# Attention and compression work moved between the tiles of the second input projection, and one compression block moved among the memory steps of layer 0

## The chip, the cores and the metric

The program runs on one core of one Trainium2 chip. Its time is the device time in microseconds; lower is better. TensorE (PE) multiplies, and its weight loads (PEld) run beside the products; VectorE (DVE), ScalarE (ACT) and GpSimd (POOL) do the rest; SyncE (SP), ACT and POOL start DMAs. All data are float32, and one matrix product of float32 leaves two records in the trace, a transpose one.

## The reference

One step of a decoder with two layers, for a prompt of 256 tokens and 8 samples of 4 new tokens (T = 288 columns together). In both layers a token mixer runs beside a four-head attention into 256 memory tokens; one projection feeds both, one projection closes them, and a SwiGLU channel mixer follows.

```python
mkv_p = mem_kv_proj(mem_prompt, w_mem_kv[i])
hp = rmsnorm(xp, norm_mix_pre[i])
if i % N_MIXERS == 0:
    mp, hl_p = s5_mixer(hp, h0_p, mkv_p, ...)      # z = hp @ w_in, then a complex scan over time
else:
    mp, (kc, ks, kw) = nsa_prompt(hp, mkv_p, ...)
    ms, (sc, ss, sw) = nsa_sample(hs, mkv_s, ...)
xp = xp + rmsnorm(mp @ w_out[i], norm_mix_post[i])
xp = xp + rmsnorm(swiglu_ffn(rmsnorm(xp, norm_ffn_pre[i]), ...), norm_ffn_post[i])
```

The second layer's attention has three branches, added with gates that the projection gives. For a sample they are:

```python
proj = cmp_subblock_proj(past_cmp, w1)             # 8 x 2048 cached rows, from pages
ckv = cmp_tokens(proj, pe, w1, b1, w2)             # 127 compressed tokens each
o_cmp, p = cmp_attend(q, q_pos, ckv, slopes)
tok = block_tokens(select_blocks(p, q_pos, total)) # 16 blocks of 64 cached rows
o_slc = slc_attend(q, q_pos, tok, kv_sel, slopes)  # over the selected cached rows
o_win = win_attend(q, q_pos, kv_w, k_pos, slopes)  # over the last 512 rows
```

## The kernel before

Each engine has its own instruction stream, written out by hand in program order, and semaphores join them. Nothing is reordered at run time: an instruction that waits holds up all that stands behind it on its engine. The eight PSUM banks (BK) are kept by a small class: `banks.fill(pe, key, b)` makes TensorE wait until bank b was read, `banks.take(eng, key)` makes a reader wait until it is full, and `wait_given` waits until a reader has let it go.

`gemm` computes one projection tile by tile: a tile is 128 output columns by 288 tokens, 8 products (16 records), and after tile number i it calls `hook(i)`. The weights come in slabs of two tiles through three slots of `W_`. `IN_ORDER` gives the order of the tiles: in layer 1 the tiles 15 and 16 are the memory queries, 0 to 5 the queries, 6 to 8 the rows to be compressed, 9 to 14 keys and values, 17 the gates. VectorE evacuates each tile (`in_evac`), scaled by the norm's inverse root, which it computes by a reciprocal after `pre_sum(4)`, and `pre_sum(4)` stands after the second tile. Layer 0 uses banks 4 and 5 for the tiles (`bank45`), layer 1 banks 4, 5 and 6 (`bank456`). `mem_step(l, zq, n)`, n = 0 to 9, is the attention into the memory in ten steps, put between the tiles.

Layer 0. After the projection come `s5_blocks` (L644), memory steps 7 (L583), 8 (L595) and 9 (L605) with `cmp_bias` (L652), then sixteen blocks `compress(b, c)` (L694, 16 products, 32 records each), which compress the cached pages of the samples for layer 1. Between the blocks stand `s5_in(n)` (L664) and `s5_y(n)` (L677) for the 15 units of the scan, whose other parts run on VectorE and GpSimd. SyncE loads the pages of sample b into half b % 2 of the buffer `AR` (16 DMAs, L2010); the first half also held `PEP`, the scratch of the position products that GpSimd sums for `cmp_bias`, and so SyncE waits for `pe_summed` first. The second half is free once memory step 8 is through (`("mo", 0, 2)`).

Layer 1. After the projection's 18 tiles come, on TensorE: the gates' transposes (L834), `compress_prompt` (L849, 64 products, 128 records), the row gates (L861), transposes of values (L868), the compressed tokens (L874, L879), scores of the prompt against them (L892), and transposes of their probabilities (L902). Then a loop over 12 units of the prompt's attention (scores L922, transposes L933, products with the values L946 to L953), with one of 12 groups of page scores (`page_scores(c, h)`, L967) of the samples in each unit. Behind the loop stand the samples' own rows (L986, L992), their compressed scores (L998), window scores (L1007), importance (L1012), transposes (L1017, L1025, L1060) and the products with values (L1039): first compressed and window values, which end in `win_used`, then four pairs of samples with the values of their pages, and last the output transposes (L1087).

Key pages come in four chunks c, each 16 DMAs on SyncE and 16 on GpSimd (L397), into two halves of `AR` (`KP`); chunk c waits until the page scores of chunk c - 2 are through. Value pages come in eight batches b of 16 DMAs (L403), even b on SyncE, odd b on GpSimd, each into its place `VAL[b]` when `wait_value_slot` says that it is free. Window keys `WK` (L2060) and values `WV` (L2062) take halves of `AR` too.

## Time and profile before

| | us |
|---|---|
| runs, median of 3 | 1201.52 |
| runs, all | 1195.62, 1201.52, 1202.44 |
| the profiled execution, its own time | 1197.44 |
| its span | 1195.8 |
| TensorE busy in the span | 1109.1 (93%) |

The span is what the profiler saw from the first to the last instruction; 1.6 us lie around it. The mean granted TensorE clock is 0.958 of its full rate. The projections, the compression and the two channel mixers are long stretches in which TensorE has no gap. Its gaps lie in the stretch from 70 to 85 us of layer 0, and between 704 and 884 us of layer 1.

### The profile page before, as it was taken

How to read it: one execution, taken by the hardware profiler on the slowest of the kernel's cores; microseconds unless marked ns; L12 is line 12 of the kernel's file. 1: busy time of each engine (PE TensorE's matmuls, PEld its weight loads, DVE VectorE, ACT ScalarE, POOL GpSimd, SP SyncE). 2: the span in 40 equal slices, each digit the busy share in tenths (PEclk: the TensorE clock that was granted, in tenths of full speed). 3: DMA queues.
4: the chain of work that ended last, by engine and by line, in shares of the span. 5: the costliest groups of instructions: out<-in, count | busy, mean ns of one | idle time of the engine just before them, and what ended most of it. 6: DMA issues, size and time to landing. Idle time of an engine off the chain costs nothing.

```text
span 1195.8 us, 16402 instructions
## 1 busy us (share of the span) xinstructions
PE 1109.1 (93%) x6032; PEld 810.3 (68%) x6032; DVE 366.4 (31%) x789; ACT 202.5 (17%) x497; POOL 242.1 (20%) x314
## 2 busy tenths in 40 slices
PE   6979999999989999999999996884888999999996
PEld 5746666666767777777767774443766777777774
DVE  5728677430142111100032104777213211110002
ACT  3310000012231000000031103554103100000000
POOL 0608567620001111130000031414400110110000
PEclk9979999999999999999999996897879999999998
DMA  8565434330425656674433344575723244333341
GB/s 321 211 211 172 144 120 121 106 107 8 175 71 186 238 217 245 263 252 153 156 141 106 109 147 125 156 267 146 211 86 122 106 141 140 130 127 113 130 145 64
DMA packets 59112, 185.13 MB, mean 155 GB/s; under 512 B 8609, under 2 KB 39586, under 8 KB 48418
## 3 DMA queue, kind: packets, MB, share of 16 engines
q1 hardware_dynamic: 52322, 165.28, 40.2%
q0 software_dynamic: 6144, 12.59, 3.6%
q10 hardware_dynamic: 576, 6.29, 1.4%
q8 instruction: 48, 0.79, 0.3%
q14 instruction: 22, 0.18, 0.0%
HBM read 180.35 MB, written 10.02 MB: 159 GB/s over the span
## 4 chain that ended last, share of the span: by engine, by line
PE 87%; DVE 4%; issue 2%; SPq 2%; DMA 2%; ACT 1%; POOLq 0%; POOL 0%; DVEq 0%
PE banks L718 29%; PE banks L496 16%; PE banks L758 14%; PE banks L694 14%; PE banks L516 3%; SPq L397 1%; PE banks L664 1%; PE banks L1039 1%; PE banks L849 1%; PE banks L677 1%; PE banks L562 1%; PE banks L1060 1%; SPq L393 1%; DMA phase<-in_slcv 1%; PE banks L471 1%
## 5 line engine op out<-in xcount | busy, mean ns | idle before, releaser
L718 PE MATMUL banks<-normed,slabs 128*128 128x288 f32 x1408 | 346.6, 410 | 9.1 <-ACT normed L1140 9.1
L718 PEld LDWEIGHTS banks<-normed,slabs 128*128 128x128 f32 x1408 | 270.1, 192 | 85.2 <-issue 10.0
L758 PE MATMUL banks<-hidden,slabs 128*128 128x288 f32 x704 | 171.2, 406 | 1.4 <-issue 1.4
L694 PE MATMUL banks<-arena,phase 128*128 128x384 f32 x512 | 171.7, 494 | 0.0
L758 PEld LDWEIGHTS banks<-hidden,slabs 128*128 128x128 f32 x704 | 133.6, 190 | 39.0 <-issue 2.3
L694 PEld LDWEIGHTS banks<-arena,phase 128*128 128x128 f32 x512 | 96.9, 192 | 65.4 <-issue 1.8
L1425 POOL TENSOR_TENSOR projected<-projected,rstd 128x288 f32<-128x288 f32 x44 | 34.9, 792 | 449.3 <-ACT projected L1207 449.3
L496 PE MATMUL banks<-normed,slabs 128*128 128x288 f32 (+1 forms) x416 | 106.6, 410 | 1.2 <-ACT normed L1140 1.2
L496 PEld LDWEIGHTS banks<-normed,slabs 128*128 128x128 f32 (+1 forms) x416 | 75.7, 187 | 27.1 <-issue 3.7
L1509 DVE TENSOR_TENSOR normed<-normed 128x288 f32<-128x288 f32 x24 | 11.0, 459 | 199.0 <-ACT normed L1200 199.0
L1207 ACT ACTIVATE projected<-projected 128x288 f32<-128x288 f32 x44 | 19.5, 443 | 281.4 <-DVE projected L1556 281.4
L496 PE MATMUL banks<-mixed,slabs 128*128 128x288 f32 x256 | 64.3, 414 | 1.3 <-DVE mixed L1942 1.3
L1561 DVE TENSOR_TENSOR hidden<-projected,banks 128x288 f32<-128x288 f32 x44 | 20.0, 454 | 138.8 <-PE banks L718 130.1
L496 PEld LDWEIGHTS banks<-mixed,slabs 128*128 128x128 f32 x256 | 49.7, 195 | 15.3 <-issue 1.4
L1556 DVE TENSOR_TENSOR projected<-banks,rstd 128x288 f32<-128x288 f32 x44 | 20.1, 457 | 127.8 <-PE banks L718 127.7
L1200 ACT ACTIVATE normed<-banks 128x288 f32<-128x288 f32 x32 | 13.1, 410 | 251.0 <-PE banks L758 164.2
L397 POOL DMA_DIRECT2D arena<-in_slck x64 | 33.3, 521 | 101.5 <-issue 97.2
L516 PE MATMUL banks<-slabs,mixed 128*128 128x256 f32 x128 | 30.6, 402 | 8.9 <-DMA slabs<-in_w 8.9
L1462 POOL TENSOR_TENSOR phase_small<-normed,phase 128x512 f32<-128x512 f32 (+1 forms) x15 | 17.1, 1141 | 91.9 <-DVE normed L1702 62.0
L1517 DVE RECIPROCAL rstd<-rstd 128x288 f32<-128x288 f32 x8 | 15.6, 1953 | 62.9 <-ACT rstd L1131 62.9
L516 PEld LDWEIGHTS banks<-slabs,mixed 128*128 128x128 f32 x128 | 26.0, 204 | 12.9 <-issue 8.8
L403 POOL DMA_DIRECT2D arena<-in_slcv x32 | 20.1, 630 | 43.2 <-issue 41.7
(293 smaller groups left out, 1071.7 us busy)
## 6 DMA issues: line engine op xcount, KB each, us to landing
slabs<-in_wfi SPq DMA_DIRECT2D x44, 1024.0 KB, 4.9
slabs<-in_w SPq DMA_DIRECT2D x25, 1024.0 KB, 4.8
arena<-in_cmp SPq DMA_DIRECT2D x128, 192.0 KB, 2.7
slabs<-in_wfo SPq DMA_DIRECT2D x32, 704.0 KB, 4.1
arena<-in_slck SPq DMA_DIRECT2D x64, 96.0 KB, 2.7
arena<-in_slck POOLq DMA_DIRECT2D x64, 96.0 KB, 2.5
out_win_old<-in_winold SPq DMA_DIRECT2D x8, 762.0 KB, 6.3
arena<-in_wink SPq DMA_DIRECT2D x4, 768.0 KB, 6.5
```

Of the source, the lines that this page charges most:

```text
L397: eng.dma_start(AR[lo:lo + 64, a:a + 384], page(slck_in, r)).then_inc(kpage_loaded[c % 2][parity], 16)
L403: eng.dma_start(dst, page(slcv_in, r)).then_inc(vpage_loaded[b], 16)
L496: ins = nc.tensor.matmul(BK[b][0:n_out, 0:T], wt[:, k, c * P:c * P + n_out], rhs[:, k, :], start=(k == 0), stop=(k == kc - 1))
L516: ins = nc.tensor.matmul(BK[b][:, 0:256], MEMT[:, k, t * P:t * P + P], wt[:, k, :], start=(k == 0), stop=(k == KC - 1))
L694: ins = nc.tensor.matmul(out.rearrange("p h (g s) -> p h g s", s=8), W1S[:, c, a, j, :], PG[b % 2][:, :, c * 8 + j, :, :].rearrange("p g h ...
L718: return nc.tensor.matmul(BK[2 * (u % SLOTS) + c][:, 0:T], wt[:, k, c * P:c * P + P], Hn[:, k, :], start=(k == 0), stop=(k == KC - 1), ski ...
L758: ins = nc.tensor.matmul(BK[b][:, 0:T], wt[:, k, :], HD[:, 11 * kh + k, :], start=(kh + k == 0), stop=(kh * 11 + k == 21))
L1207: A(z, z, ACT.Silu).then_inc(silu_done, 1)
L1425: tt(z, z, RST[:, :], ALU.mult).then_inc(up_done, 1)
L1462: ch.tick(tt(hr, re, cos, ALU.mult))
L1556: banks.give(tt(z, BK[2 * (u % SLOTS)][:, 0:T], RST[:, :], ALU.mult), key)
L1561: banks.give(tt(HD[:, u, :], z, BK[2 * (u % SLOTS) + 1][:, 0:T], ALU.mult), up)
```

## The change

**Layer 0.** `compress` calls `between(i)` ahead of each product but the first. Block (0, 0) now begins right after `s5_blocks`, and memory steps 7, 8, 9 and `cmp_bias` stand between its products. `s5_in(0)` follows it. `s5_in(n)` for n over 1 stands one block later than before in the count of blocks, `s5_in(1)` in the middle of block 1, and the last `s5_y` in the middle of the last block. `PEP` lies in `M_`, in twelve tiles that are summed step by step, and SyncE no longer waits for `pe_summed` before the first pages.

**Layer 1.** The tiles come in the order 15, 16, 6, 7, 8, 0 to 5, 17, 9 to 14. Between them stand the memory steps and now also `compress_prompt`, the compressed tokens and their scores and transposes, the gates, and the samples' compressed scores, window scores, importance and transposes. Banks 6 and 7 serve them, and the tiles have banks 4 and 5 (`bank45`). VectorE and ScalarE have the matching work in between. In the unit loop stand, new, the window's maximum and exponentials (units 0 and 1), its scaling (unit 2) and its five transposes (`window_turn`, units 3 to 7, in bank 7 with the page scores). The selected rows' probabilities are transposed head by head, with more of it overlapped with the exponentials.

**DMAs of layer 1.** Window keys come during the first channel mixer. Key chunk 0 waits for memory step 8 of layer 1, chunk 1 for the window scores, chunks 2 and 3 as before. Value batch 0 waits for the last `window_turn`, batches 1 and 2 for the last page scores (before, batches 0 and 1 waited for the last slabs of the projection alone), 3 to 5 for `win_used`, 6 and 7 for the transposes of the selected rows. On SyncE the window values stand behind value batch 0.

```diff
-IN_ORDER = [[6, 7, 0, 1, 2, 3, 4, 5], [15, 16] + list(range(15)) + [17]]
+IN_ORDER = [[6, 7, 0, 1, 2, 3, 4, 5], [15, 16, 6, 7, 8, 0, 1, 2, 3, 4, 5, 17] + list(range(9, 15))]
...
-        PEP = AR[:, 2048:6144].rearrange("p (c q f) -> p c q f", c=2, q=16)
+        PEP = M_[:, 0:1536].rearrange("p (n f) -> p n f", f=P)
...
-        KP = [AR[:, a:a + 6144].rearrange("p (b g h n) -> p b g h n", b=4, g=4, h=H) for a in (6144, 0)]
-
-        VAL = [W_[:, 0:3072], W_[:, 3072:6144]] + [AR[:, a:a + 3072] for a in (6144, 9216, 0, 3072)] + [KV[:, :], U[:, 0:3072]]
+        KP = [AR[:, a:a + 6144].rearrange("p (b g h n) -> p b g h n", b=4, g=4, h=H) for a in (0, 6144)]
+
+        VAL = [W_[:, 3072:6144]] + [AR[:, a:a + 3072] for a in (6144, 9216)] + [KV[:, :]] + [AR[:, a:a + 3072] for a in (0, 3072)]
+        VAL += [U[:, a:a + 3072] for a in (0, 3072)]
...
             if c >= 2:
                 banks.take(eng, ("sk", c - 2, H - 1))
             elif c == 1:
+                for h in range(H):
+                    banks.take(eng, ("sws", h))
+            else:
                 banks.take(eng, ("mo", 1, 2))
-            else:
-                banks.take(eng, ("hc", B - 1, 1))
-            lo, base = 64 * parity, 6144 * (1 - c % 2)
-            for b in pairs:
+            lo, base = 64 * parity, 6144 * (c % 2)
+            for b in range(4):
...
-            if b < 2:
-                for n in range(FIRST["out", 1] - SLOTS, FIRST["out", 1]):
-                    eng.wait_ge(*released[n])
-            elif b < 4:
-                for h in range(H):
-                    banks.take(eng, ("sws", h))
-            elif b < 7:
+            if b == 0:
+                banks.take(eng, ("swt", 4))
+            elif b < 3:
+                banks.take(eng, ("sk", 3, H - 1))
+            elif b < 6:
                 eng.wait_ge(win_used, 1)
             else:
                 banks.take(eng, ("st", NPG))
...
             s5_blocks()
-            mem_step(0, 6, 7)
-            cmp_bias()
-            mem_step(0, 6, 8)
+
+            def beside_first(i):
+                if i == 6:
+                    mem_step(0, 6, 7)
+                elif i == 7:
+                    cmp_bias()
+                elif i == 9:
+                    mem_step(0, 6, 8)
+                elif i == 13:
+                    mem_step(0, 6, 9)
+
+            compress(0, 0, between=beside_first)
             for r in range(2):
                 for part in range(2):
                     banks.wait_given(pe, ("bt", r, part))
             for m in range(8):
                 banks.wait_given(pe, ("in", 0, m))
-            mem_step(0, 6, 9)
             for key in (("ms", 0, 4), ("ms", 0, 3), ("mto", 0), ("mo", 0, 2)):
                 banks.wait_given(pe, key)
             pe.wait_ge(smat_loaded, 32)
             s5_in(0)
-            for blk in range(2 * B):
+
+            def beside_block(blk, i):
+                if i == 8 and blk == 1:
+                    s5_in(1)
+                elif i == 8 and blk == 2 * B - 1:
+                    s5_y(N_UNIT - 1)
+
+            for blk in range(1, 2 * B):
                 b, c = blk // 2, blk % 2
-                compress(b, c, halfway=lambda: s5_in(1) if blk == 0 else None)
+                compress(b, c, between=lambda i: beside_block(blk, i))
-                for n in outputs_beside(blk):
-                    s5_y(n)
-                if blk + 2 < N_UNIT:
-                    s5_in(blk + 2)
+                for n in outputs_beside(blk - 1):
+                    if n < N_UNIT - 1:
+                        s5_y(n)
+                if blk + 1 < N_UNIT:
+                    s5_in(blk + 1)
...
-                if i == 1:
-                    pre_sum(4)
-                if 3 <= i <= 12:
-                    mem_step(1, 15, i - 3)
-
-            gemm("in", 1, Hn, KC, N_NSA_SLAB, IN_ORDER[1], ready=lambda k: pe.wait_ge(h_done, 16 + k + 1), cols=36,
-                 bank=bank456, hook=beside_in)
-            banks.wait_given(pe, ("in", 1, 17))
...
+                if i == 1:
+                    pre_sum(4)
+                if 3 <= i <= 12:
+                    mem_step(1, 15, i - 3)
+                if 5 <= i <= 8:
+                    compress_prompt(i - 5)
+                if i == 9:
+                    prompt_tokens()
+                if i == 11:
+                    prompt_cmp_scores()
+                if i == 12:
+                    gates_turn()
+                    sample_cmp_scores()
+                if i == 13:
+                    row_gates()
+                if i == 14:
+                    window_scores()
+                    prompt_cmp_turn(0)
+                    prompt_cmp_turn(1)
+                if i == 15:
+                    importance()
+                    prompt_cmp_turn(2)
+                    prompt_cmp_turn(3)
+                if i == 16:
+                    sample_cmp_turn()
+                    prompt_cmp_turn(4)
+                    prompt_cmp_turn(5)
+
+            gemm("in", 1, Hn, KC, N_NSA_SLAB, IN_ORDER[1], ready=lambda k: pe.wait_ge(h_done, 16 + k + 1), cols=36,
+                 bank=bank45, hook=beside_in)
...
+                if 3 <= n < 8:
+                    window_turn(n - 3)
...
+                if n == 1:
+                    row_exp(lambda h: SW[:, h, :], 3, sw_max, 1, sw_exp)
...
+                if i == 10:
+                    query_rows()
+                if i == 11:
+                    prompt_cmp_scored()
+                if m >= 9 and m < 15:
+                    upper_keys(m)
+                if i == 12:
+                    prompt_cmp_prob()
+                    sample_cmp_scored()
+                if i == 13:
+                    row_gates_out()
+                    sample_cmp_prob()
+                if i == 15:
+                    selection()
             for g in range(G):
...
+                    ch.step(V.tensor_reduce(NEWMAX, SNEW, AX_X, ALU.max))
+                    V.tensor_reduce(NS[:, 3:6], SW, AX_X, ALU.max, negate=True).then_inc(sw_max, 1)
...
-            sp.wait_ge(pe_summed, 1)
             load_pages(0)
...
-                    load_key_pages(sp, SP, 0, 0, [u // 2])
+                    a = 6144 + 1536 * (u // 2)
+                    sp.dma_start(AR[:, a:a + 1536], wink_in[u // 2]).then_inc(wink_loaded, 16)
             load_stage("mem", 1, N_MEM_SLAB)
-            load_stage("in", 1, N_NSA_SLAB)
+            for u in range(N_NSA_SLAB):
+                load(FIRST["in", 1] + u)
+                if u == 3:
+                    store_mem_kv(1)
+            load_key_pages(sp, SP, 0, 0)
+            load_key_pages(sp, SP, 1, 0)
             for m in range(6, 15):
                 banks.wait_given(sp, ("in", 1, m))
             sp.dma_start(kv_out, Z_[:, 6 * T:15 * T]).then_inc(kv_stored, 16)
-            store_mem_kv(1)
-            sp.wait_ge(memkv_stored, 32)
-            load_key_pages(sp, SP, 1, 0)
+            load_key_pages(sp, SP, 2, 0)
+            load_key_pages(sp, SP, 3, 0)
             wait_value_slot(sp, 0)
             load_value_pages(sp, SP, 0)
-            for c in range(2, 4):
-                load_key_pages(sp, SP, c, 0)
             banks.take(sp, ("sk", 2, H - 1))
-            for b in range(4):
-                a = 6144 + 1536 * b
-                sp.dma_start(AR[:, a:a + 1536], wink_in[b]).then_inc(wink_loaded, 16)
-            banks.take(sp, ("sk", 3, H - 1))
             sp.dma_start(AR[:, 0:6144], winv_in).then_inc(winv_loaded, 16)
...
-            load_key_pages(pool, POOL, 0, 1)
             banks.take(pool, ("fo", 0, KC - 1))
             query_blocks(1, 15)
-            load_key_pages(pool, POOL, 1, 1)
-            wait_value_slot(pool, 1)
-            load_value_pages(pool, POOL, 1)
-            for c in range(2, 4):
+            for c in range(4):
                 load_key_pages(pool, POOL, c, 1)
-            for b in range(3, B, 2):
+            for b in range(1, B, 2):
                 wait_value_slot(pool, b)
                 load_value_pages(pool, POOL, b)
             channel_mixer(1)
```

TensorE in layer 0, from `s5_blocks` (L644) on; the products of `compress` are the rows with `128x3x128`. Before:

```order
L644 MATMUL banks<-cst,cmp_kv 128x128 x12
L583 MATMUL banks<-cst,hidden 128x128 x2
L652 MATMUL banks<-cst,phase_small 128x1 x2
L595 MATMUL banks<-arena,hidden 32x128 x32
L605 MATMUL banks<-cst,hidden 128x128 x4
L664 MATMUL banks<-projected,hidden 128x64 x16
L694 MATMUL banks<-arena,phase 128x3x128 x8
L664 MATMUL banks<-projected,hidden 128x64 x16
L694 MATMUL banks<-arena,phase 128x3x128 x8
```

and now:

```order
L645 MATMUL banks<-cst,cmp_kv 128x128 x12
L695 MATMUL banks<-arena,phase 128x3x128 x6
L584 MATMUL banks<-cst,hidden 128x128 x2
L695 MATMUL banks<-arena,phase 128x3x128
L653 MATMUL banks<-cst,phase_small 128x1 x2
L695 MATMUL banks<-arena,phase 128x3x128 x2
L596 MATMUL banks<-arena,hidden 32x128 x32
L695 MATMUL banks<-arena,phase 128x3x128 x4
L606 MATMUL banks<-cst,hidden 128x128 x4
L695 MATMUL banks<-arena,phase 128x3x128 x3
L665 MATMUL banks<-projected,hidden 128x64 x16
L695 MATMUL banks<-arena,phase 128x3x128 x8
```

Block (0, 0) has moved from behind `s5_in(0)` (L664, now L665) to the place right behind `s5_blocks`, and the memory steps (L584, L596, L606) lie inside it.

TensorE in layer 1, the first four tiles of the projection (L496, now L497) with what they wait for; L471 (now L472) is `pre_sum(4)`. Before:

```order
L496 MATMUL banks<-normed,slabs 128x288 [waits normed_done,bank4_free,slab2_loaded]
L496 MATMUL banks<-normed,slabs 128x288 [waits normed_done] x7
L496 MATMUL banks<-normed,slabs 128x288 [waits bank5_free]
L496 MATMUL banks<-normed,slabs 128x288 x7
L471 MATMUL banks<-projected,cst 128x288 [waits squares_summed,bank7_free]
L496 MATMUL banks<-normed,slabs 128x288 [waits bank6_free,slab0_loaded]
L496 MATMUL banks<-normed,slabs 128x288 x7
L496 MATMUL banks<-normed,slabs 128x288 [waits bank4_free]
L496 MATMUL banks<-normed,slabs 128x288 x7
```

and now:

```order
L497 MATMUL banks<-normed,slabs 128x288 [waits normed_done,bank5_free,slab2_loaded]
L497 MATMUL banks<-normed,slabs 128x288 [waits normed_done] x7
L497 MATMUL banks<-normed,slabs 128x288 [waits bank4_free]
L497 MATMUL banks<-normed,slabs 128x288 x7
L472 MATMUL banks<-projected,cst 128x288 [waits squares_summed,bank7_free]
L497 MATMUL banks<-normed,slabs 128x288 [waits bank5_free,slab0_loaded]
L497 MATMUL banks<-normed,slabs 128x288 x7
L497 MATMUL banks<-normed,slabs 128x288 [waits bank4_free]
L497 MATMUL banks<-normed,slabs 128x288 x7
```

The third tile waited for bank 6, which no earlier tile had filled; now it waits for bank 5, that of the first tile.

SyncE in layer 1, around the window values. Before, they stand behind the window keys and ahead of value batch 2:

```order
L2060 DMA arena<-in_wink 128x1536 [waits bank7_full]
L2060 DMA arena<-in_wink 128x1536 x3
L2062 DMA arena<-in_winv 128x6144 [waits bank7_full]
L400 UNCONDITIONAL_BRANCH [waits bank4_full,bank3_full,bank2_full]
L400 ISA
L361 TENSOR_LOAD pages
L361 ISA x8
L403 ISA
L403 DMA arena<-in_slcv 128x192
```

and now, from the last DMA of a group of value batch 0 on:

```order
L406 DMA slabs<-in_slcv 128x192
L403 REGISTER_ALU
L403 COMPARE_AND_BRANCH
L2172 DMA arena<-in_winv 128x6144 [waits bank7_full]
L403 UNCONDITIONAL_BRANCH [waits bank7_full]
L403 ISA
L363 TENSOR_LOAD pages
L363 ISA x8
L406 ISA
L406 DMA arena<-in_slcv 128x192
```

Value batch 0 has moved in ahead of the window values, behind the last key pages.

## Rows read from the trace of the kernel before

**Rows 1.** The page's chain that ended last: shares of the span by engine.

```profile
PE 87%; DVE 4%; issue 2%; SPq 2%; DMA 2%; ACT 1%; POOLq 0%; POOL 0%; DVEq 0%
```

**Rows 2.** Waits of TensorE, whole span: total us, times, longest us.

```profile
PE banks L1060 <- DVE phase L1924: 9.6, 3, 4.0
...
PE banks L902 <- DVE params L1786: 5.6, 1, 5.6
```

**Rows 3.** Timeline of TensorE, layer 0: start us, duration us, line, idle before.

```profile
72.68 0.44 PE L583 MATMUL banks<-cst,hidden 128*128 128x128 f32 x2 [1.78 <-DVE hidden L1547]
...
77.80 1.94 PE L595 MATMUL banks<-arena,hidden 128*32 128x128 f32 x32 [3.12 <-DMA arena<-in_memv]
...
84.69 7.49 PE L694 MATMUL banks<-arena,phase 128*128 128x384 f32 x16
...
98.51 1.12 PE L664 MATMUL banks<-projected,hidden 32*128 32x64 f32 x32
...
99.56 10.59 PE L694 MATMUL banks<-arena,phase 128*128 128x384 f32 x32
```

**Rows 4.** Timeline of SyncE's DMA issues, layer 0.

```profile
25.86 9.30 SPq L1978 DMA_DIRECT2D slabs<-in_w  x2
...
59.26 15.47 SPq L2010 DMA_DIRECT2D arena<-in_cmp  x16
...
81.56 14.90 SPq L2010 DMA_DIRECT2D arena<-in_cmp  x16
```

**Rows 5.** Stretches of 1 us, L849 alone: PE busy, PEld busy, PEclk, DMA.

```profile
711.00:712.00 1.00, 1.00 (x22) 1.00 (x22) 1.00 0.05 16
...
716.00:717.00 1.00, 1.00 (x13) 1.00 (x12) 0.50 0.43 121
```

**Rows 6.** Timeline of VectorE at the second projection's first tiles.

```profile
632.85 1.96 DVE L1517 RECIPROCAL rstd<-rstd 128x288 f32<-128x288 f32 x1 [4.84 <-ACT rstd L1131]
...
634.83 0.82 DVE L1568 SCALAR_TENSOR_TENSOR projected<-banks,rstd 128x288 f32<-128x288 f32 x2
```

**Rows 7.** Timeline of TensorE, layer 1, projection to window scores.

```profile
632.11 7.92 PE L496 MATMUL banks<-normed,slabs 128*128 128x288 f32 x32
...
708.76 9.59 PE L849 MATMUL banks<-projected,phase 64*128 64x45 f32 x128
...
739.78 0.34 PE L922 MATMUL banks<-projected 64*128 64x128 f32 x1 [1.18 <-ACT hidden L1305]
...
749.95 1.59 PE L967 MATMUL banks<-arena,phase 128*32 128x512 f32 x8
...
786.47 1.06 PE L967 MATMUL banks<-arena,phase 128*32 128x512 f32 x8 [0.37 <-DMA arena<-in_slck]
...
801.27 0.83 PE L986 MATMUL banks<-cst,projected 128*32 128x128 f32 x6
...
804.66 2.76 PE L1007 MATMUL banks<-arena,phase 128*32 128x512 f32 x24
```

**Rows 8.** Timeline of SyncE's DMA issues, layer 1.

```profile
729.08 13.98 SPq L403 DMA_DIRECT2D slabs<-in_slcv  x16
...
753.13 31.42 SPq L397 DMA_DIRECT2D arena<-in_slck  x32
```

**Rows 9.** DMA issues by line: KB each, median us to landing.

```profile
arena<-in_winv SPq DMA_DIRECT2D x1, 3072.0 KB, 10.1
```

**Rows 10.** Timeline of GpSimd, issues of the last value pages.

```profile
848.24 2.47 POOL L403 DMA_DIRECT2D phase<-in_slcv  x4 [2.62 <-issue]
...
860.87 2.47 POOL L403 DMA_DIRECT2D phase<-in_slcv  x4 [1.74 <-issue]
```

**Rows 11.** Timeline of TensorE, value products of layer 1.

```profile
822.04 5.41 PE L1039 MATMUL banks<-arena,hidden 128*48 128x192 f32 x64
...
870.15 0.53 PE L1039 MATMUL banks<-cmp_kv,hidden 128*48 128x192 f32 x1 [5.74 <-DMA phase<-in_slcv]
```

More of the change, by code:

```diff
@@ new lines, in importance, with sample_cmp_turn @@
+            def importance():
+                pe.wait_ge(imp_done, 1)
+                banks.fill(pe, "imp", 3)
+                banks.filled(nc.tensor.matmul(BK[3][:, 0:96], c2("same"), IMP[:, :, 0:32], start=True, stop=True), "imp")
+            def sample_cmp_turn():
+                pe.wait_ge(sc_prob, 1)
+                banks.wait_given(pe, "imp")
+                banks.fill(pe, "sct", 3)
+                for h in range(H):
+                    ins = nc.tensor.transpose(BK[3][0:NCMP, P * h:P * h + P], PC[:, h, 0:NCMP], ident)
+                banks.filled(ins, "sct")
@@ L905, in _ @@
+            for j in range(6):
+                ins = nc.tensor.matmul(BK[4][:, 32 * j:32 * j + 32], Q0[0:64, j % 3, :], Z[0:64, 9 + j, TP:T], start=True, stop=True)
+            banks.filled(ins, "snew")
             for n in range(6):
@@ new lines, in _ @@
+                ins = V.tensor_copy(dst, src.rearrange("p h (b t) -> p h b t", b=B))
+                if g < 3:
+                    ch.step(ins)
+            ins.then_inc(q_done, 1)
+            for h in range(H):
+                banks.take(dve, ("sws", h))
+                banks.give(stt(SW[:, h, 0:WIN], c2("win_d"), slope[:, h:h + 1], BK[h][:, :], ALU.mult, ALU.add), ("sws", h))
+            banks.take(dve, "snew")
+            for j in range(6):
+                dst = SNEW[:, j, :] if j < 3 else SW[:, j - 3, WIN:WIN + 32]
+                ins = stt(dst, c2("new_d"), slope[:, j % 3:j % 3 + 1], BK[4][:, 32 * j:32 * j + 32], ALU.mult, ALU.add)
+                if j < 5:
+                    ch.tick(ins)
+                else:
+                    banks.give(ins, "snew")
@@ L1925, in _ @@
[L1925 to L1927 removed]
+                if n == 2:
+                    dve.wait_ge(sw_exp, 1)
+                    ch.step(V.reciprocal(SS[:, 3:6], SS[:, 3:6]))
+                    ch.step(tt(SS[:, 3:6], SS[:, 3:6], GR[:, 6:9], ALU.mult))
+                    for h in range(H):
+                        ins = ts(SW[:, h, :], SW[:, h, :], SS[:, 3 + h:4 + h], None, ALU.mult)
+                        if h < 2:
+                            ch.tick(ins)
+                    ins.then_inc(sw_prob, 1)
@@ new lines, in slc_prob, with slc_turned @@
+            def slc_prob(h):
+                dve.wait_ge(ss_exp, h + 1)
+                ch.step(V.reciprocal(SS[:, h:h + 1], SS[:, h:h + 1]))
+                ch.step(tt(SS[:, h:h + 1], SS[:, h:h + 1], GR[:, 3 + h:4 + h], ALU.mult))
+                ts(S_SLC[:, h, :], S_SLC[:, h, :], SS[:, h:h + 1], None, ALU.mult).then_inc(ss_prob, 1)
+            def slc_turned(h):
+                for q in range(1, 4, 2):
+                    banks.take(dve, ("st", h, q))
+                    dst, src = turned_tiles(h, q)
+                    banks.give(V.tensor_copy(dst, src), ("st", h, q))
```

598 lines of the change are left out of this document (298 added, 300 removed).

## The prediction, made blind

> **What bounds the kernel now.** The page's chain that ended last comes first: 87% of it is TensorE, DVE, issue and DMA have 2 to 4% each [rows 1]. So an edit pays only where it removes a wait of TensorE, shortens TensorE's own work, or shortens a transfer for which TensorE waits. TensorE is busy for 1109.1 us of 1195.8. The waits of TensorE by partner show where to look: 9.6 us for the probabilities of the selected rows and 5.6 us for those of the prompt's compressed tokens [rows 2]. Then the timelines: layer 0 from 70 to 100 us [rows 3, 4], the second projection with what follows it [rows 5 to 7], and the chain of page DMAs up to the last value products [rows 7 to 11].
>
> **Layer 0.** Both kernels reach the end of `s5_blocks` alike, at 72.68 - 1.78 = 70.9. Before, block 1 begins at 99.56 [rows 3]: 28.7 us, in which stand block (0, 0), memory steps 7 to 9, `cmp_bias` and three calls of `s5_in`. TensorE idles in it for 1.8 us ahead of step 7 and for 3.1 ahead of step 8 (memory values landing), and some 2 us more around them. The first half of the block, 16 records, takes 7.49 us, where a whole block of 32 takes 10.59 later, so it runs at less than full rate too. The same work without gaps, at the later rate: 10.59 for the block, 3 x 1.12 for `s5_in` (two of these now stand later, but they still count), 0.44 for step 7, 1.94 for step 8 (its row, perhaps too high, as it follows a gap), and 1.0 for step 9 and `cmp_bias` (small products, by the same rows). That is 17.3, so 28.7 - 17.3 = **11.3 us gained**.
>
> What must hold for it. The pages of sample 0 must be there at 71: SyncE is through with the slabs at 25.86 + 9.30 = 35, and 16 pages take 15.5 to issue [rows 4]; as `pe_summed` no longer holds them, they end at about 54. Step 7 wants what VectorE gives at 72.6; with six products of 0.66 ahead of it, it comes at 74.9. Step 8 wants the memory values, which land at 77.8; it comes at about 78.6, behind nine products. This margin is 1 us. The second half of the pages waits for step 8, now done at about 81.4; with 14.9 of issue [rows 4] and some 2.6 to land it is whole at 99. Blocks 0 and 1 end at 88.2 + 11.7 = 99.9, a margin of 1 again, and a miss costs the difference, up to 3. The scan keeps its distance, three blocks from `s5_in(n)` to `s5_y(n)`, and the last output has half a block, 5.3, to hide it. The summing of `PEP` on GpSimd goes to another buffer in the same steps: nothing. The term is 8 to 12.
>
> **Layer 1, the projection.** Five parts.
> First, a new wait. With two banks the third tile waits until VectorE has evacuated the first, and that needs the reciprocal, done at 632.85 + 1.96 = 634.8, and half of 0.82 [rows 6]: 635.3, where it began at 632.11 [rows 7]. 3.2 us. TensorE has stood for some microseconds then, and it may start at the lower of its two levels; the bound is 0 to 3, and I take 2.5, since rows after other gaps do so. Together +5.7.
> Second, `compress_prompt` takes 9.59 us for 128 records [rows 7]. In its first microseconds the granted clock is 1.00 and 22 records fit in one, later it is 0.50 and 13 fit in one, with PE and PEld both fully busy [rows 5]. Between full tiles I expect the first: 128/22 = 5.8, so -3.8.
> Third, from its end at 718.35 to the loop's first scores at 739.78 there are 21.4 us. The waits of 5.6 [rows 2] and 1.2 [rows 7] go: -6.8.
> Fourth, the rest, 14.6, runs at the lower level. At the full one it takes between 7.3 (all of it clocked) and 14.6; I take 9: -5.7.
> Fifth, what comes in from behind the loop: the window scores, 2.76 [rows 7], compressed scores, samples' rows, importance and transposes, some 3.4, and half a microsecond of waits for banks 6 and 7: +6.7.
> Sum: 5.7 - 3.8 - 6.8 - 5.7 + 6.7 = -3.9. The loop begins at 735.9.
>
> A rule of the Trainium skill speaks against the second and fourth parts. The page "TensorE: Matmul & The Clock Gate", section "HAM oscillation — how this bites in real kernels", puts the loss of clock down to gaps in which TensorE idles. By that rule alone small products back to back would keep the full clock wherever they stand, and moving them would not bring those 9.5 us; the clock in the row for 716 us, where no gap is, does not bear it out [rows 5]. By the rule the projection part would come out at +5.6 and not at -3.9.
>
> **Layer 1, from the loop on.** Now the page DMAs count. In the loop VectorE gets the window's maximum (1632 wide, about 2.1 in unit 0) and the scaling in unit 2; I add 0.6 up to the end of the page scores of unit 2. That end is 749.95 + 1.59 = 751.5 now, 11.8 behind the loop's start [rows 7], and 748.3 after. Call it P2; from it the distances are fixed by issuing:
> - chunks 2 and 3 are issued from P2 + 1.6 for 31.4 [rows 8], up to P2 + 33; the scores of unit 9 wait for them at P2 + 35, as before [rows 7]; the loop ends at P2 + 49.8 (801.27 now), and I keep that;
> - behind them SyncE now issues value batch 0, 14.0 [rows 8], and only then the window values, at P2 + 47; they take 10.1 [rows 9]: P2 + 57.4;
> - TensorE, done with the loop at P2 + 50 and with little left that was not moved, waits there for 4 to 6 us, new. The window products take 5.4 to 8 (64 records take 5.41 [rows 11]): `win_used` at P2 + 65, about 813;
> - GpSimd has batch 1 from the last page scores, P2 + 43.7, on. A batch there is four groups of 4.2 (from 848.24 to 860.87 are three [rows 10]): 16.8. Batches 3, 5 and 7 wait for `win_used`: 65 + 2 x 16.8 = 98.6, then 12.6 to the last group, 2.5 for it, 2.6 to land: P2 + 117, that is **865.3**.
> Before, the last pair begins at 870.15, after 5.74 of idle [rows 11], though its last group was out at 863.3 [rows 10], 6.8 earlier. The slabs for the output projection were loading beside it. With the earlier place of window and value batches I take 2.6, the usual distance of the other groups; with 6.8 the pair begins at 869.5. So this part gives **4.5**, between 0 and 9. The 9.6 us for the selected probabilities [rows 2] may go, but only in front of this wait, so I book nothing for them; were the pages not last, they would be the gain.
>
> For that landing the page "DMA: Bandwidth & Descriptors" of the Trainium skill, section "Anatomy of one DMA — SWDGE (gpsimd) path", has a formula of a fixed 2.0 us and the bytes over 436 GB/s: an estimate of 2.2 for the 96 KB of such a page. The 6.8 of the trace is three times that, so the last transfer was not alone. With 2.2 for 2.6 the sum would move by 0.4.
>
> Nothing else in the diff touches the end; the channel mixers are unchanged. The window keys come during the first one, where DMA queues have room: nothing, and 2 us if that is wrong.
>
> **The sum.** -11.3 - 4.5 = -15.8: the profiled execution goes from 1197.44 to 1181.6. It lies 4.1 under the median; the mean of the three runs is 1199.9, and I predict against that: **1184**. Its own bounds, 8 and 12 for the first term, 0 and 9 for the second, with the spread of the runs, give 1177 to 1191.
>
> **The rivals.**
> - Better: the pages are not last. If the clock stays up through the projection (-10 and not -4) and the value pages take fewer than 16.8 a batch on GpSimd, the 9.6 us count as well: -22, 1178. For it: SyncE needs only 14.0 for a batch [rows 8]. Against it: GpSimd's own pitch is even over four groups [rows 10].
> - Layer 1 gives nothing: the last landing takes 6.8 again, or the projection gains nothing: the small products hold their clock down also between tiles, or the bank wait comes back with every tile. Layer 0 alone is -11: 1189.
> - Small products run at one rate wherever they stand, and only idle gaps lower the clock: then the second and fourth part of the projection give nothing, -15.8 + 9.5 = -6.3: 1194. For it: the clock was 1.00 at 711 us. Against it: 0.50 at 716, with no gap [rows 5]. This is what the clock page's rule, above, would make of it.
> - Layer 0 does not deliver: memory values or pages come 3 us late at each of both margins, and the clock stays low behind the gap: 4 to 5 gained, 1193 with a little less in layer 1.
> - Slower: the window values. Now they are issued while GpSimd's pages of batch 1 land, and three later batches hang on `win_used`. Should they take 31 us, like the 3 MB of the key chunks [rows 8], and not 10.1 [rows 9], `win_used` comes 21 later, the last pair at 886, and the sum is +16 - 11 = +5: 1205; with TensorE at its lower level in such a wait, 5 to 9 more, up to 1214. It decides from `win_used` at 829 on. Against it: one large transfer in few descriptors, and 16 us of slack.
>
> **How the numbers follow.** The forecast has 0.50, better 0.15, no gain in layer 1 0.15, one rate for small products 0.05, layer 0 late 0.07, slower 0.08. One per cent, 12 us, is about what a measurement of this kernel can tell from no change; that is 1188. Faster: 0.43 of the forecast's 0.50, all of the better case, 0.04 of the third: 0.62. Slower by 1% needs over 1212, 0.05 with what no case names. The rest is 0.33. The range goes from 1173, the better case with its spread, to 1197; it leaves out the slower case and tails.
>
> **What would show it.** Right: block (0, 0) directly behind `s5_blocks`, and no wait for `in_memv`; one idle time of 3 to 6 us ahead of the third tile, ended by VectorE; a granted clock near 1.00 through the projection; the scores of unit 9 waiting for `in_slck`; a wait for `in_winv` behind the loop; and the last pair waiting for `in_slcv` near 854 in the new time (865.3 - 11.3). Wrong: waits for `in_cmp` ahead of block 2, clocks of 0.5 between the tiles, `win_used` over 10 us later than P2 + 65, or last value products that wait for the probabilities and not for pages. Times of layer 1 in this text are on the old clock, without the 11.3 of layer 0.

## The result and the profile after

The changed kernel takes 1191.83 us in the median of 17 runs (1189.99 to 1196.2), the kernel before 1197.62 (17 runs, 1195.62 to 1203.32). The ratio is 0.9947, with a 95% interval of 0.9935 to 0.996: 6.3 us faster (4.8 to 7.8). The forecast gain was 16. The profiled execution took 1191.83 us with a span of 1190.2, against 1197.44 and 1195.8; the mean granted clock is 0.965 (0.958 before).

The timeline of TensorE, changed kernel, layer 0 (start us, duration, line, operation, idle before). Against them stand [rows 3].

```profile
71.33 4.04 PE L695 MATMUL banks<-arena,phase 128*128 128x384 f32 x12
...
77.90 1.95 PE L596 MATMUL banks<-arena,hidden 128*32 128x128 f32 x64
...
84.94 1.12 PE L665 MATMUL banks<-projected,hidden 32*128 32x64 f32 x32
...
279.60 17.68 PE L497 MATMUL banks<-projected,slabs 128*128 128x288 f32 x72
```

Block (0, 0) stands directly behind `s5_blocks`, step 8 waits for nothing, and the block is through at 84.94. The gated projection behind the blocks begins at 279.60. In the kernel before, this row of the same view is

```profile
290.68 17.68 PE L496 MATMUL banks<-projected,slabs 128*128 128x288 f32 x72
```

so layer 0 gave 11.1 us up to there. Before, the second projection begins at

```profile
621.94 9.85 PE L496 MATMUL banks<-normed,slabs 128*128 128x288 f32 x32 [1.20 <-ACT normed L1140]
```

The same view of the changed kernel in layer 1, from the second projection to the output projection; [rows 7, 11] answer to them.

```profile
611.92 9.85 PE L497 MATMUL banks<-normed,slabs 128*128 128x288 f32 x32 [1.20 <-ACT normed L1202]
...
625.41 9.69 PE L497 MATMUL banks<-normed,slabs 128*128 128x288 f32 x32 [3.16 <-DVE projected L1641]
...
646.09 2.00 PE L851 MATMUL banks<-projected,phase 64*128 64x45 f32 x32
...
690.56 5.83 PE L497 MATMUL banks<-normed,slabs 128*128 128x288 f32 x16
...
727.52 0.37 PE L1006 MATMUL banks<-hidden,projected 64*128 64x128 f32 x1
...
733.91 1.07 PE L1049 MATMUL banks<-arena,phase 128*32 128x512 f32 x8 [2.93 <-DVE phase L1969]
...
740.46 1.87 PE L1049 MATMUL banks<-arena,phase 128*32 128x512 f32 x8
...
804.27 6.72 PE L1094 MATMUL banks<-arena,slabs 128*48 128x192 f32 x64 [7.62 <-DMA arena<-in_winv]
...
852.65 8.11 PE L1094 MATMUL banks<-arena,hidden 128*48 128x192 f32 x64 [14.08 <-DMA arena<-in_slcv]
...
864.59 7.09 PE L1094 MATMUL banks<-phase,hidden 128*48 128x192 f32 x64 [3.37 <-DMA phase<-in_slcv]
...
878.10 27.18 PE L497 MATMUL banks<-mixed,slabs 128*128 128x288 f32 x103 [1.30 <-DVE mixed L2054]
```

The reader is to see: the idle time ahead of the third tile (625.41); four calls of `compress_prompt` of 2 us between tiles (the first is shown); one tile that takes 5.83 us where its neighbours take 4.15 (the granted clock is 0.76 from 690 to 697); the page scores of unit 2, P2, ending at 740.46 + 1.87 = 742.3; 7.6 us for the window values; and the last pair at 864.59. Before, it began at 870.15 [rows 11]. So of the 11.1 us of layer 0 only 5.6 reach the last pair: layer 1 took the rest back. Where, the queues show. SyncE's issues, changed kernel (start, time from the first to the last issue, count), beside [rows 8]:

```profile
743.94 32.14 SPq L400 DMA_DIRECT2D arena<-in_slck  x32
777.85 14.84 SPq L406 DMA_DIRECT2D slabs<-in_slcv  x16
792.91 0.36 SPq L2172 DMA_DIRECT2D arena<-in_winv  x1
795.04 32.80 SPq L406 DMA_DIRECT2D arena<-in_slcv  x32
829.77 13.91 SPq L406 DMA_DIRECT2D phase<-in_slcv  x16
```

and GpSimd's, the first group of batch 3 and the last of batch 7, beside [rows 10]:

```profile
813.17 2.47 POOL L406 DMA_DIRECT2D cmp_kv<-in_slcv  x4 [9.18 <-issue]
...
860.29 2.47 POOL L406 DMA_DIRECT2D phase<-in_slcv  x4 [1.75 <-issue]
```

GpSimd stands for 9.2 us ahead of batch 3, until the window products (804.27 + 6.72 = 811.0) are through, and then issues three batches one right behind the other. The chain of layer 1 is: page scores of unit 2, key pages, value batch 0, window values, window products, three batches on GpSimd, last pair. From the key pages on, the window products are all that TensorE has in it.

### The profile page after: what moved, and what is told of

Same layout as the page of the kernel before. It is cut to its first block, busy times and chain, and to the rows that moved or that the text cites. A ratio compares the mean times of both kernels' runs of the same rounds, so it can differ in the third digit from the quotient of the medians.

```text
span 1190.2 us, 16408 instructions
## 1 busy us (share of the span) xinstructions
PE 1102.9 (93%) x6032; PEld 806.8 (68%) x6032; DVE 366.9 (31%) x789; ACT 201.6 (17%) x496; POOL 241.7 (20%) x315
## 4 chain that ended last, share of the span: by engine, by line
PE 86%; issue 4%; SPq 3%; DVE 3%; DMA 2%; POOLq 1%; ACT 1%; POOL 0%; DVEq 0%
PE banks L719 29%; PE banks L497 16%; PE banks L759 14%; PE banks L695 14%; PE banks L517 3%; SPq L400 2%; PE banks L665 1%; PE banks L1094 1%; POOLq L363 1%; DMA arena<-in_winv 1%; PE banks L678 1%; PE banks L563 1%; SPq L406 1%; DVE rstd L1590 1%; SPq L396 1%
## 5 line engine op out<-in xcount | busy, mean ns | idle before, releaser
L497 PE MATMUL banks<-normed,slabs 128*128 128x288 f32 (+1 forms) x416 | 111.2, 424 | 4.4 <-DVE projected L1641 3.2
L497 PEld LDWEIGHTS banks<-normed,slabs 128*128 128x128 f32 (+1 forms) x416 | 78.9, 194 | 29.6 <-issue 6.4
L497 PE MATMUL banks<-mixed,slabs 128*128 128x288 f32 x256 | 64.4, 415 | 1.3 <-DVE mixed L2054 1.3
L497 PEld LDWEIGHTS banks<-mixed,slabs 128*128 128x128 f32 x256 | 49.8, 195 | 15.4 <-issue 1.4
L1262 ACT ACTIVATE normed<-banks 128x288 f32<-128x288 f32 x32 | 13.1, 410 | 270.5 <-PE banks L759 164.2
L1094 PE MATMUL banks<-arena,hidden 128*48 128x192 f32 x128 | 20.4, 396 | 17.7 <-DMA arena<-in_slcv 14.1
```

The lines of the kernel that those rows point to most:

```text
L497: ins = nc.tensor.matmul(BK[b][0:n_out, 0:T], wt[:, k, c * P:c * P + n_out], rhs[:, k, :], start=(k == 0), stop=(k == kc - 1))
L1094: return nc.tensor.matmul(out, probs[:, 48 * b:48 * b + 48], values, start=first, stop=last, skip_group_check=True)
```

## The experiments

Changes in us are the ratio times 1197.6. Intervals of the ratios are 0.0012 to 0.0019 to either side, 1.4 to 2.3 us, so a difference between two changed kernels is known to about 2.5 us. Where a difference to the changed kernel is given, it is one of two ratios to the kernel before.

**The two layers apart.** `l0_only` is the kernel before with the layer-0 hunks of the diff (`compress` with `between`, `beside_first`, `beside_block`, `PEP` in `M_`, no wait for `pe_summed`); `l1_only` is the changed kernel without them.

> The kernel before with the part of the change in layer 0 alone. Theory A (the two parts add up, and the profile reads layer 0 as 11.1 us and layer 1 as a loss of some 5 with the rest of the span): 10 to 11 us faster than before, ratio 0.991, with the layer-1 stretch moved as a whole. Rival B (the page DMAs of layer 1 do not care when layer 0 ends, or the clock gives part of it back): 6 us or less, as much as the whole change brings, so that layer 1 is neutral.

Measured: 0.9907 (0.9893 to 0.992), -11.1 us.

> The changed kernel with layer 0 as it was. Theory A: 4 to 5 us slower than before, ratio about 1.004, because the distance from the page scores of unit 2 to the last value pair grew from 118.7 to 122.3 us and the distance ahead of it did not shrink enough. Rival B: within 1 us of the kernel before.

Measured: 1.0031 (1.0019 to 1.0044), +3.7 us. Its span is 1.6 us longer than before, the smaller end of what the runs show. So layer 0 brings all of the gain and more, layer 1 is a loss; -11.1 + 3.7 = -7.4 agrees with -6.3 within the intervals. Rival B of both expectations is out.

**What the last pair hangs on.** Two kernels that differ from the changed one in one place each.

```diff
 # winv_first
+            banks.take(sp, ("sk", 2, H - 1))
+            sp.dma_start(AR[:, 0:6144], winv_in).then_inc(winv_loaded, 16)
             wait_value_slot(sp, 0)
             load_value_pages(sp, SP, 0)
-            banks.take(sp, ("sk", 2, H - 1))
-            sp.dma_start(AR[:, 0:6144], winv_in).then_inc(winv_loaded, 16)
```

> The changed kernel with the window values issued ahead of value batch 0 on SyncE. Theory A (window values set the time of win_used, and three batches of GpSimd hang on it): window values land at about 788 in place of 804, GpSimd goes from its batch 1 into batch 3 without a gap at about 805, and the last pair begins 7 us earlier, near 857.5: about 7 us faster than the changed kernel, ratio to before about 0.989. Rival B (TensorE's own work and the landing of pages under load set the end, not the issue): the window products come earlier and the last pair moves by 2 us or less.

Measured: 0.9881 (0.9865 to 0.9897), -14.3 us, 7.9 faster than the changed kernel. Its GpSimd and its TensorE:

```profile
801.32 2.47 POOL L406 DMA_DIRECT2D arena<-in_slcv  x4 [1.73 <-issue]
805.50 3.05 POOL L406 DMA_DIRECT2D cmp_kv<-in_slcv  x4 [1.71 <-issue]
```

```profile
796.65 5.41 PE L1094 MATMUL banks<-arena,slabs 128*48 128x192 f32 x64
...
857.35 6.97 PE L1094 MATMUL banks<-phase,hidden 128*48 128x192 f32 x64 [9.40 <-DMA phase<-in_slcv]
```

The window products wait for nothing, batch 3 follows batch 1 at once (805.50 where it was 813.17), and the last pair begins at 857.35, where 857.5 was expected. The chain starts 0.9 us earlier in this trace (P2 ends at 741.47), so 6.4 of the 7.2 us lie behind P2.

```diff
 # batch3_early
+            elif b == 3:
+                eng.wait_ge(kv_used, 1)
             elif b < 6:
                 eng.wait_ge(win_used, 1)
...
-                seq_pv(b, PCT[0:NCMP, :], VC[0:NCMP, b, :], first=b // 2 % 2 == 0)
+                ins = seq_pv(b, PCT[0:NCMP, :], VC[0:NCMP, b, :], first=b // 2 % 2 == 0)
+            ins.then_inc(kv_used, 1)
```

> The changed kernel with value batch 3 released by the compressed products alone (a semaphore of its own) and not by the window products. Theory A: GpSimd starts batch 3 at about 805 in place of 813, nothing else moves up to the window products, and the last pair begins 7 us earlier, ratio to before about 0.989, like the run that moves the window values. If instead the late landing of the window values matters in itself (theory C: TensorE stands 7.6 us for them and everything of TensorE behind comes later), this run gains little and that one gains.

Measured: 0.9902 (0.9887 to 0.9917), -11.7 us, 5.4 faster than the changed kernel; the last pair begins at 856.60. TensorE still idles 6.5 us for the window values there, and the last pair is as early as in `winv_first`: theory C is out. The gains of the two, 5.4 and 7.9 us, do not differ clearly. What counts is when GpSimd may go on, not when TensorE gets the window values.

**More of the same lever.** `swap_queues` has `for b in (0, 3, 5, 7)` on GpSimd, `for b in (1, 2, 4, 6)` behind the window values on SyncE, and `kv_used`.

> The changed kernel; GpSimd issues value batches 0, 3, 5 and 7 (batch 0 is free after the last window turn), SyncE the window values and then 1, 2, 4 and 6, and batch 3 waits for the compressed products alone. Theory A (issue slots decide): GpSimd begins batch 0 at 776 behind its key pages and ends batch 7 near 846, SyncE ends near 847, the last pair begins near 849 in place of 864.6: 15 us faster than the changed kernel, ratio to before about 0.982. Rival B (below some 857 the landing of 96 KB pages or TensorE's pairs take over): 857, as in the two runs with one edit, ratio 0.988.

Measured: 0.9854 (0.9837 to 0.9871), -17.5 us; the last pair begins at 854.40, between the two forecasts. GpSimd was through at 846.8, as theory A has it, but SyncE only at 838.70 + 13.90 = 852.6: three batches from 787.94 took 48.8 us, 16.3 each with the pauses between them, and not 14. The bound was again an issue queue, the other one. The next kernel, `balanced`, takes this up: `(0, 1, 3, 5)` and four pages of 7 on GpSimd, `(2, 4, 6)` and twelve pages of 7 on SyncE.

> The changed kernel with value batches 0, 1, 3, 5 and the first four pages of 7 on GpSimd, and the window values, 2, 4, 6 and the other twelve pages of 7 on SyncE; batch 3 waits for the compressed products alone. Theory A: with SyncE at 16.3 us a batch from 788 on (as the run with the swapped queues shows it) and GpSimd at 16.8 from 775 on, the last page is issued at about 849 on either queue and the last pair begins near 851: 13 to 14 us faster than the changed kernel, 3 us faster than the swapped queues, ratio to before 0.983. Rival B (what is left after the swap is not the issue but TensorE and the landing): no faster than the swapped queues, 0.985.

Measured: 0.9791 (0.9772 to 0.981), -25.0 us. Its TensorE:

```profile
843.21 7.06 PE L1097 MATMUL banks<-arena,hidden 128*48 128x192 f32 x64 [9.46 <-DMA arena<-in_slcv]
...
850.65 5.41 PE L1097 MATMUL banks<-phase,hidden 128*48 128x192 f32 x64
```

The last pair follows the third without idle time and runs at the full clock, 5.41 us where it took 7.09. The pair begins 13.9 us earlier than in the changed kernel, the output projection 16.1 earlier (862.00), and the ratios are 18.7 us apart, with intervals of 2 on each. The forecast time of the pair (851) was right, the ratio of 0.983 too high. The pair came at 851 for another reason than forecast: SyncE was through at 820.20 + 26.95 = 847.2, not 849, and the pair stood behind the third, which waits for batch 5 (9.46 us) and runs at a low clock. So the queues no longer alone decide; TensorE does in part.

**The wait ahead of the third tile.**

```diff
 # third_bank
+            first_tiles = [0]
+
+            def bank645():
+                first_tiles[0] += 1
+                return 6 if first_tiles[0] == 3 else bank45()
...
-                 bank=bank45, hook=beside_in)
+                 bank=bank645, hook=beside_in)
```

> The changed kernel with bank 6 for the third tile of the second projection, all others as they are. Theory A: the idle time of 3.2 us ahead of the third tile goes, and with it the 1.8 us by which that tile and the next run long; since the chain of page DMAs starts from the unit loop, all of the 5 us arrive at the end: 5 us faster than the changed kernel, ratio to before 0.990. Rival B (that stretch is covered, a later wait in the loop takes it): 1 us or less.

Measured: 0.9891 (0.9874 to 0.9909), -13.1 us, 6.7 faster than the changed kernel. The third tile in its trace:

```profile
620.49 7.92 PE L497 MATMUL banks<-normed,slabs 128*128 128x288 f32 x32
...
683.87 4.15 PE L497 MATMUL banks<-normed,slabs 128*128 128x288 f32 x16
```

From the first tile (610.32) it begins 10.2 us later, in the changed kernel 13.5. That is 3.3 for the wait; the lower clock behind it cost another 1.8 (7.92 against 9.69 for the same 32 records). A third part comes later: the tile at 690.56 that took 5.83 us takes 4.15 here (683.87). Up to the unit loop that makes 6.8 us (108.8 for 115.6). Whether the wait caused the slow tile too stays open: `l1_only` has the wait, 13.5 us from the first tile to the third, and not the slow tile (113.7 us up to the loop). From the first tile to the last pair it is 247.3 us (610.32 to 857.66) and not 252.7, so about the 5 us forecast arrive at the end of the chain; the measured 6.7 agrees with both within its interval.

> The balanced queues together with bank 6 for the third tile. Theory A: the two gains add up, as one lies ahead of the chain of page issues and the other in it: 6 to 7 us more than the balanced queues alone, ratio to before near 0.977 (1170.5 us). Rival B: they overlap by more than 3 us, 0.980 or above.

Measured: 0.9751 (0.9734 to 0.9769), 1169.6 us in the median, -29.8 us: 4.8 more than the balanced queues alone, with intervals of 2 on each. That is less than the forecast 6 to 7 but not clearly so, and rival B (0.980 or above) is out; in the traces the last pair comes 5.6 us earlier (845.10 for 850.65). It is the fastest kernel of the study, 23.5 us ahead of the changed one.

**The window's work in the unit loop.** `window_later` takes the maximum (L1997) behind the page scores of unit 1, and the exponentials, the scaling and the five `window_turn` one unit later each.

> The changed kernel with the maximum, exponentials, scaling and transposes of the window one unit later in the loop of units (the maximum after the page scores of unit 1). Theory A: TensorE's wait for bank 7 at unit 1 (2.9 us, ended by VectorE) goes by 2, the page scores of unit 2 end 2 us earlier, and the chain of issues and the last pair come 2 us earlier: ratio to before about 0.993. Rival B (VectorE is full in every unit of the loop, so the same work one unit later costs the same there): within 0.5 us of the changed kernel.

Measured: 0.9973 (0.9961 to 0.9985), 3.1 us slower than the changed kernel. Neither theory had this. Its SyncE and its GpSimd:

```profile
740.93 37.09 SPq L400 DMA_DIRECT2D arena<-in_slck  x32
```

```profile
763.63 2.35 POOL L400 DMA_DIRECT2D arena<-in_slck  x4 [8.77 <-PE banks L1060]
```

P2 did come earlier, 739.3 for 742.3, of which 1.3 are there from the first tile on (610.65), and chunk 2 came with it. But chunk 3 waits for the page scores of unit 5, and those now lay behind VectorE's scaling, a wait of 2.6 us in unit 4 and the lower clock behind it: they began at 759.71, in the changed kernel at 757.32. The two chunks took 37.09 us and not 32.14, and the chain behind them came later. So not P2 alone, but units 2 and 5 both hold the queue.

**The clock in small products.** `prompt_block` calls the four parts of `compress_prompt` together at i = 8; `prompt_two` calls two at i = 6 and two at i = 8.

> The changed kernel with the four parts of the prompt's compression, 128 records, together behind the ninth tile of the second projection, not in four places. Theory A (at the full clock these products need 22 records a microsecond, as before, and each of the four places costs a change-over of 0.4 us): 5.8 us from first to last start, about 1.5 us less than in four parts. Rival B (among full tiles they run at 17 a microsecond whatever the grouping): 7.3 us, nothing gained. Rival C: so long a run of small products pulls the granted clock down, and the block takes 9.6 us as before: 2 us slower than the changed kernel.

Measured: 0.9964 (0.995 to 0.9978), 2.0 us slower than the changed kernel, which is no more than its uncertainty; the traces have 118.2 us from the first tile to the unit loop where it was 115.6. The stretches of this line alone (TensorE busy, weight loads busy, granted clock, DMA share, GB/s):

```profile
665.00:666.00 1.00, 1.00 (x22) 1.00 (x22) 1.00 0.00 0
666.00:667.00 1.00, 1.00 (x20) 1.00 (x20) 0.86 0.00 0
667.00:668.00 1.00, 1.00 (x14) 1.00 (x12) 0.50 0.00 0
```

The block takes 9.68 us. Rival C is borne out: the clock falls from 2.4 to 1.2 GHz in the middle of it, at 666.7, with TensorE busy all the time; full tiles and 1.6 us of memory products stand right ahead. It is still low in the tile behind, which takes 6.74 us.

The numbers behind the x are not a rate. They count every record that runs in the stretch, also those that began before it, and at 1.00 one record takes 0.29 us: over the ten stretches of the whole block the counts add up to 169, for 128 records.

> The changed kernel with the prompt's compression in two stretches of 64 records, behind the seventh and the ninth tile. As one stretch of 128 between tiles the clock fell to 0.50 after some 4.5 us; as four of 32 it stayed at 1.00. If the small products themselves pull the clock down when they last long, two stretches of 64 (3 us each) still stay at 1.00 and take 6.2 us together; if the clock falls in them, over 7.5.

One run with a profile, 1190.27 us: 3.6 and 3.7 us from the start of each stretch to the next tile, at a granted clock of 1.00 throughout. The clock held, as in the first branch, but the sum is 7.3 and not 6.2. That is the true rate at 1.00: 64 records in 3.6 us, 56 ns each, or 17.7 in a microsecond. The 6.2, like the 22 of the first expectation, rests on the counts. The four parts of the changed kernel take 7.6 (646.09 to 648.02 is the first). So a change-over costs less than 0.2 us.

## Why the prediction was wrong, step by step

The direction was right and the time lies in the range of 1173 to 1197, but the gain is 6.3 us and not 16, and under the 1% to which I gave 0.62. Against 1184 the time is 7.8 us off and the gain 9.5, mainly because I predicted from the mean of three runs, 1199.9, and the kernel before has 1197.6 in 17. The bound was read rightly: TensorE, and in layer 1 the chain of page DMAs. Each step in its own order:

| step | forecast | measured |
|---|---|---|
| layer 0 | -11.3 | -11.1 (279.60 for 290.68); run alone -11.1 |
| start of the second projection | 610.6 | 611.92 |
| projection up to the unit loop | -3.9 | -2.2 (115.6 us for 117.8) |
| loop's start to P2 | 12.4 | 14.8 |
| P2 to the window values' issue | 47 | 50.6 |
| P2 to their landing | 57.4 | 61.9 |
| P2 to `win_used` | 65 | 68.7 |
| P2 to batch 3 on GpSimd | 65 | 70.8 |
| P2 to the last pair | 117 | 122.3 |

On the new clock the last pair was forecast for 854.0 and begins at 864.6. The 10.6 us are 1.3 + 1.7 + 2.4 + 5.3 (each rounded): the start of the projection, the projection, the loop to P2, and P2 to the last pair.

Three sums of the forecast do not come out. 98.6 + 12.6 + 2.5 + 2.6 is 116.3, not 117. From 865.3 to 870.15 are 4.9 us, not 4.5; with 116.3 it would have been 5.5, further from the result. And 1199.9 - 8 is 1192, so the upper bound of 1191 was too low.

**Layer 0: right**, in its size and in both margins. The changed kernel lost 1.1 us of it again before the second projection: from the gated projection to that it takes 332.3 us, the kernel before 331.3 and `l0_only`, in which the window keys do not come during the channel mixer, 331.4 (278.28 to 609.72). The window keys do not cost this: `winv_first`, `swap_queues`, `balanced` and `third_bank` have them in the channel mixer too and take 331.4. Single profiles differ by as much.

**The wait for the bank: right**, 3.16 us forecast as 3.2 and 1.8 for the clock taken as 2.5. `third_bank` shows that the step was a real loss of the change. What the forecast did not have is the slow tile at 690.56, 1.7 us. The projection as a whole missed by 1.7 as well: `compress_prompt` brought 1.8 too little, the bank cost 0.8 less (4.9 for 5.7), and the rest came out 1.0 better.

**`compress_prompt` at the full clock: mis-sized by a misread row.** 128/22 = 5.8 us took the x22 of [rows 5] for a rate, and it counts the records that overlap the microsecond. At 17.7 in a microsecond 128 records take 7.2 us, and the four calls take 7.6, so the term was -2.0 and not -3.8. The clock in these four stretches was as forecast, 1.00, and the rival that small products run at one rate wherever they stand is out: 9.6 us in one block, 7.3 and 7.6 in pieces. This answers the doubt about the rule of the Trainium skill, "TensorE: Matmul & The Clock Gate", section "HAM oscillation — how this bites in real kernels": idle gaps are not the only thing that lowers the clock, as the block of `prompt_block` falls from 1.00 to 0.50 without one.

**The loop to P2: mis-sized.** I added 0.6 us for VectorE's window work. The maximum over 1632 columns stands in unit 0 ahead of the evacuation of the page scores, TensorE waits 2.93 us for their bank (733.91), and the next products run at the lower clock (0.50 from 736 to 742; in the kernel before it is 1.00 from 740 to 746). The term was 3.0.

**From P2 to the last pair: the step that turned the sign.** The mechanism was right, the batches on GpSimd behind `win_used` included, and `winv_first` and `batch3_early` show it by moving the pair by 7.2 and 8.0 us. The size was wrong, and most parts of it in the same direction. A row of 14.0 us for a batch runs from the first issue to the last; ahead of each batch its engine stands another 2 (776.1 to 777.85, 827.8 to 829.77 on SyncE; 811.0 to 813.17 on GpSimd), which I left out twice, ahead of batch 0 and ahead of batch 3: 1.8 and 2.2 us. The chunks and batch 0 took 1.6 us longer than in [rows 8] (32.14 and 14.84), the window values 11.3 and not 10.1, the three batches on GpSimd 0.9 more. Two parts were shorter: the window products took 6.7 where the forecast left 7.6, and the last landing 1.8 for 2.6. So 117 became 122.3, where the kernel before has 118.65 [rows 7, 11]. `l0_only`, with the layer 1 of the kernel before, has 120.3 (738.83 to 859.10), so single profiles differ by almost 2 us here. The forecast gain of 4.5 us of layer 1 was a loss of 3.7 (2.3 to 5.3 by the interval) when it was run alone.

**The rivals.** "Slower: the window values" named the right place, but the size between: counted from P2, `win_used` came 3.7 us late and batch 3 5.8, not 21. "Better: the pages are not last" was far off; the last pair still waits 3.4 us for pages. The rival of one rate for small products gave -6.3, 1194, and -6.3 was measured. That is luck: its ground is out, as the clock stayed at 1.00 in the four stretches and the term brought 2.0 us, and the loss lay behind the projection. "Layer 0 alone, -11" had the right layer, and even that was too good, since it took layer 1 for neutral. In the range I let the part from the loop on run from 0 to 9 and never below, though three of its terms had no allowance for a delay; with +4 on that side the forecast's own bounds, 1177 to 1191, would have reached to 1195.

That the last landing takes 2.6 us and not 6.8 was right (860.29 + 2.47 to 864.59 is 1.8), but the 6.8 went to batch 5 (issued at 843.42 + 2.47, its pair begins at 852.65), beside the output slabs that SyncE issued from 843.93 on.

## What to carry to other kernels

When work of the bounding engine is moved ahead, look first at the queue that feeds it later: here 11 us were gained on TensorE and 4 to 5 of them were lost in layer 1, where one more batch hung on one late semaphore; two lines moved in the issue order gave back about as much as the whole change had brought. A count of records in a stretch is not their rate when they overlap; take the rate from start times. Write a chain of DMAs out with the time between the groups, not only inside them, and give each link a bound on the late side. And a wait of a few microseconds put in front of a long stretch costs more than itself, as the clock behind it is lower.

## What the hardware showed beyond that

- Of products of 45 columns, 128 records in one stretch brought the granted clock from 1.00 to 0.50 with no idle time, while two stretches of 64 or four of 32 between full tiles kept it at 1.00.
- At 1.00 such records follow each other every 56 ns (64 in 3.6 us), at 0.50 every 107 (42 records of the kernel before start from 713.6 to 718.0). One record lasts 0.29 us at 1.00 and 0.40 at 0.50.
- Between two batches of 16 pages SyncE issues nothing for 2 us (from 795.04 + 32.80 to 829.77 are 1.9), and GpSimd goes on 2.2 us after the products for which it waited.
